# Value projection by rows in four PSUM banks, first weights and activations side by side on one queue, linear-attention head output in the fourth bank

## What is computed

```python
def rmsnorm(x, g):
    xf = x.astype(jnp.float32)
    y = xf * lax.rsqrt(jnp.mean(xf * xf, axis=-1, keepdims=True) + RMS_EPS)
    return (y * g.astype(jnp.float32)).astype(x.dtype)
...
    qkv = jnp.einsum('bsd,de->bse', h, w_qkv).reshape(B, S, 3, N_HEADS, HEAD_DIM)
    q, k, v = qkv[:, :, 0], qkv[:, :, 1], qkv[:, :, 2]
...
    att = jnp.einsum('bnthd,bnshd->bnhts', q_d, k_d)      # linear attention, 4 heads
    att = jnp.where(causal, att, jnp.zeros_like(att))
    o_intra = jnp.einsum('bnhts,bnshv->bnthv', att, v)
...
        o = jnp.einsum('bthd,bhdv->bthv', qc, state)
    o = o_intra + o_inter.transpose(1, 0, 2, 3, 4)
```

## Time and profile before

| what | us |
|---|---|
| median of three runs | 992.41 (991.16 to 992.53) |
| the profiled execution, whole time | 992.35 |
| its span (first to last instruction) | 991.0 |
| PE busy | 982.0, 99% of the span; the chain that ended last is 99% PE |
| DVE busy | 673.7, 68% |
| ACT busy | 578.8, 58% |
| POOL busy | 67.1, 7% |
| DMA, mean over the span | 182 GB/s |

### The profile page before, as it was taken

The page is one execution under the profiler, slowest core; times in us unless marked ns, Lnnn a source line. Parts: engine busy times, 40 slices in busy tenths (PEclk is TensorE's granted clock), DMA queues, the critical chain, the costliest instruction groups (busy, mean ns, idle before and its releaser), DMA issues.

```text
span 991.0 us, 13369 instructions
## 1 busy us (share of the span) xinstructions
PE 982.0 (99%) x5158; PEld 830.4 (84%) x5158; DVE 673.7 (68%) x1143; ACT 578.8 (58%) x1014; POOL 67.1 (7%) x80
## 2 busy tenths in 40 slices
PE   9999999999999999999999999999999999999997
PEld 6887788888888998888888888888888777888886
DVE  6867776655667888766566678778577344667564
ACT  6677755444547896645454575557675434575443
POOL 2223110000000250000000000000120000000000
PEclk9999999999999999999999999999999999999999
DMA  9753545555555445555555556455543433335551
GB/s 368 284 193 139 176 170 204 200 204 179 201 181 174 167 170 177 181 195 186 217 185 198 186 196 228 173 199 181 186 153 129 170 128 132 124 127 197 185 191 43
DMA packets 27263, 180.32 MB, mean 182 GB/s; under 512 B 3008, under 2 KB 3904, under 8 KB 6464
## 3 DMA queue, kind: packets, MB, share of 16 engines
q1 hardware_dynamic: 26336, 176.89, 50.1%
q0 software_dynamic: 288, 2.10, 0.6%
q10 hardware_dynamic: 576, 0.47, 0.2%
HBM read 178.40 MB, written 1.05 MB: 181 GB/s over the span
## 4 chain that ended last, share of the span: by engine, by line
PE 99%; DVE 0%; ACT 0%; issue 0%; DVEq 0%
PE bank L324 25%; PE bank L279 16%; PE bank L281 16%; PE bank L280 16%; PE bank L332 13%; PE bank L294 1%; PE bank L433 1%; PE bank L449 1%; PE bank L552 1%; PE bank L722 1%; PE bank L481 1%; PE bank L295 1%; PE bank L461 1%; PE bank L492 1%; PE bank L425 1%; PE bank L667 0%
## 5 line engine op out<-in xcount | busy, mean ns | idle before, releaser
L1286 DVE TENSOR_TENSOR lo<-raw,hi 128x1024 fp32r<-128x1024 f32 x318 | 376.8, 1231 | 19.3 <-ACT hi L793 19.3
L793 ACT ACTIVATE hi<-raw 128x1024 fp32r<-128x1024 f32 x318 | 320.3, 1050 | 96.0 <-PE bank L281 95.6
L324 PE MATMUL bank<-X,hi 128*128 128x512 f32 x1016 | 266.9, 395 | 0.0
L324 PEld LDWEIGHTS bank<-X,hi 128*128 128x128 f32 x1016 | 185.1, 189 | 33.3 <-issue 0.4
L332 PEld LDWEIGHTS bank<-X,lo 128*128 128x128 f32 x1016 | 138.5, 190 | 10.1
L332 PE MATMUL bank<-X,lo 128*128 128x256 f32 x1016 | 141.6, 282 | 0.0
L824 ACT ACTIVATE bt<-bank 128x256 f32<-128x256 f32 x135 | 51.1, 380 | 147.6 <-PE bank L324 139.4
L1300 DVE TENSOR_TENSOR zr<-bank,bt 128x256 f32<-128x256 f32 x64 | 27.2, 424 | 108.9 <-ACT bt L824 108.9
L279 PE MATMUL bank<-hi,zh 128*128 128x512 f32 x256 | 100.0, 390 | 0.0
L281 PE MATMUL bank<-hi,zl 128*128 128x512 f32 x256 | 99.8, 390 | 0.0
L280 PE MATMUL bank<-lo,zh 128*128 128x512 f32 x256 | 99.6, 389 | 0.0
(11 more groups left out here) (308 smaller groups left out, 1375.8 us busy)
## 6 DMA issues: line engine op xcount, KB each, us to landing
raw<-in_w SPq DMA_DIRECT2D x64, 1024.0 KB, 4.8
raw<-in_rin SPq DMA_DIRECT2D x8, 1024.0 KB, 4.7
raw<-in_wk SPq DMA_DIRECT2D x4, 1024.0 KB, 8.5
raw<-in_wq SPq DMA_DIRECT2D x4, 1024.0 KB, 6.9
raw<-in_wo SPq DMA_DIRECT2D x4, 1024.0 KB, 4.7
raw<-in_mk SPq DMA_DIRECT2D x4, 1024.0 KB, 4.7
raw<-in_mv SPq DMA_DIRECT2D x4, 1024.0 KB, 4.8
raw<-in_rout SPq DMA_DIRECT2D x4, 1024.0 KB, 4.8
```

What stands on the lines that cost most here:

```text
L324: return PE.matmul(bank[b][:, :], wh[:, c:c + P], x[:, k_, :, :].rearrange("p a b -> p (a b)"), start=k_ == 0, stop=k_ == NC - 1, skip_gro ...
L793: ACTE.activation(hi[u_ % HIS][:, c], raw[u_ % RAW][:, c], ACT.Copy).then_inc(hi_cut, 1)
L1286: DVE.tensor_tensor(lo[u_ % RAW][:, c], raw[u_ % RAW][:, c], hi[u_ % HIS][:, c].bitcast(F32), ALU.subtract).then_inc(lo_cut, 1)
```

## The change

It does five things.

1. **Layout.** The `wv` tiles are cut by rows: tile i holds input rows 256 i to 256 i + 255 with all 1024 value columns. For the first four chunks of 128 input rows a new array `front` holds 256 columns of x and 1024 columns of weights side by side. It comes into four tensors `front[0..3]` by five DMAs on SP's queue (384, 256, 640, 640 and 640 KB), then x's chunks 4 to 7 in one DMA, then most of `vec`. Of `vec` only the eight gain columns that the first step reads come on ACT's queue.
2. **Value projection.** `first_rows` takes the place of `first_tokens`: per chunk of input rows twelve matmuls, into banks 0 to 3. `rows` takes the place of `tokens` for tiles 2 and 3. The four value results thus finish together, after the last tile. `wk` 0 and `wq` 0 go to banks (4, 5) and (7, 6).
3. **Order.** ACT cuts the high part of tile 3 before it squares any chunk (before: four squares first). `total` stands on the PE behind all 96 matmuls of the projection (before: 12 ahead of the end). DVE evicts all four results after it has cut the low parts of tiles 4 and 5. `vec_in` is waited for after the squares.
4. **Start.** `warm` is cleared by POOL, and two matmuls run on it instead of four.
5. **Linear attention.** `g_second` writes bank 3, and ACT reads it from there.

The core of the diff:

```diff
-            for k_ in range(4):
-                w, kk = slice(k_ * 512, (k_ + 1) * 512), 4 * t + k_
-                p.wait_ge(first_hi, kk + 1)
+            for j in range(4 * t, 4 * t + 4):
+                kk, c = j // 2, j % 2
+                w = slice(j % 4 * 512, j % 4 * 512 + 512)
+                p.wait_ge(first_hi, j + 1)
                 p.wait_ge(x_low, low_at("mix0", kk))
                 for s_ in range(2):
+                    b = 2 * c + s_
                     if kk == 0:
-                        fill(("wv", 0, s_), banks[s_])
+                        fill(("wv", b), b)
...
         p.wait_ge(warm_set, 1)
-        for i in range(4):
+        for i in range(2):
             PE.matmul(bank[7][:, :], warm[:, 0:P], warm[:, :], start=True, stop=True)
 
-        first_tokens(0, (4, 5))
-        first_tokens(1, (4, 5))
-        tokens("wv", 2, X, (0, 1))
-        tokens("wv", 3, X, (0, 1), (0,))
+        first_rows(0)
+        first_rows(1)
+        for i in (2, 3):
+            rows("wv", i, 4, xh[:, 2 * i:2 * i + 2, :], xl[:, 2 * i:2 * i + 2, :])
         p.wait_ge(ones_in, 16)
         total("mix0", 0)
-        tokens("wv", 3, X, (0, 1), (1,))
         p.wait_ge(ident_in, 16)
-        cols("wk", 0, X2, (2, 3))
-        cols("wq", 0, X2, (4, 5))
-        p.wait_ge(*free["wv", 1, 1])
+        cols("wk", 0, X2, (4, 5))
+        cols("wq", 0, X2, (7, 6))
+        for b in range(4):
+            p.wait_ge(*free["wv", b])
...
-            done = fill(("go", n), 0)
+            done = fill(("go", n), 3)
...
-        ACTE.dma_start(vec[:, :], A["vec"]).then_inc(vec_in, 16)
+        ACTE.dma_start(vec[:, 0:NC], A["vec"][:, 0:NC]).then_inc(gain_in, 16)
         ACTE.preload_act_table_set(LOGS)
+        a.wait_ge(gain_in, 16)
+        for j in range(8):
+            a.wait_ge(first_in[(0, 1, 2, 2, 3, 3, 4, 4)[j]], 16)
+            if j % 2 == 0:
+                high(x_of[j // 2], xh, "norm_mix", j // 2)
+            c, e = j % 4 * 512, S + j % 2 * 512
+            ACTE.activation(hi[j // 4][:, c:c + 512], front[j // 2][:, e:e + 512], ACT.Copy).then_inc(first_hi, 1)
+        a.wait_ge(x_in, 16)
+        for j in (4, 5):
+            high(x_of[j], xh, "norm_mix", j)
+        hi_to(2 * 2 + 2)
+        for j in (6, 7):
+            high(x_of[j], xh, "norm_mix", j)
+        hi_to(2 * 3 + 2)
+        for j in range(NC):
+            square("mix0", x_of, j)
         a.wait_ge(vec_in, 16)
...
-        hi_to(2 * 2 + 2)
-        for j in range(4):
-            square("mix0", hx, j)
-        hi_to(2 * 3 + 2)
-        for j in range(4, NC):
-            square("mix0", hx, j)
...
-        lo_to(2 * (T_OF["wk", 0] + 1))
+        lo_to(2 * (T_OF["wq", 0] + 1))
         by_token("mix0", 1)
         d.wait_ge(tok_made, 1)
-        to_v(0)
-        lo_to(2 * (T_OF["wq", 0] + 1))
-        to_v(1)
+        for n in range(4):
+            s_, r = half_of(n % 2, n // 2)
+            d.wait_ge(*full["wv", n])
+            DVE.tensor_scalar(v[:, s_, r], bank[n][:, :], nst[:, NST["mix0"] + s_:NST["mix0"] + s_ + 1],
+                              None, ALU.mult).then_inc(free["wv", n][0], 1)
...
-        for n in range(3):
-            piece(n)
-            half_tile(n)
-        half_tile(3)
+        for n, (k_, c, e) in enumerate(((0, 0, 3 * S), (0, 3 * S, 5 * S), (1, 0, 5 * S), (2, 0, 5 * S), (3, 0, 5 * S))):
+            SP.dma_start(front[k_][:, c:e], A["front"][:, k_, c:e]).then_inc(first_in[n], 16)
+        SP.dma_start(hx[:, 4:NC, :], A["xT"]).then_inc(x_in, 16)
+        SP.dma_start(vec[:, NC:NV], A["vec"][:, NC:NV]).then_inc(vec_in, 16)
         load(2)
```

More of the change, by code:

```diff
@@ L190, in build @@
     mh, ml = M2[:, :, 0, :], M2[:, :, 1, :]
+    front = [slot("front0", 10, [5 * S]), slot("front1", 10, [5 * S], off=20 * S), slot("front2", 10, [5 * S], off=40 * S),
+             slot("front3", 5, [5 * S])]
+    x_of = [f_[:, 0:S] for f_ in front] + [hx[:, j, :] for j in range(4, NC)]
     q, k, v = slot("q", 5), slot("k", 6), slot("v", 7, [2, D])
@@ L906, in act @@
         at_tile("wv", 2)
+        at_tile("wv", 3)
         inverse_root("mix0")
[L908 removed]
         a.wait_ge(mem_in, 16)
         for j in range(NC):
[L911 removed]
+            high(mem[:, j, :], mh, "g_mem_2", j)
         at_tile("wk", 0)
@@ L941, in act @@
                 if 4 <= j < 8:
-                    square("mem", mem, 2 * (j - 4) + e)
+                    square("mem", [mem[:, n, :] for n in range(NC)], 2 * (j - 4) + e)
         a.wait_ge(*full["av", 7])
@@ L1165, in g_second @@
             a.wait_ge(*full["go", n])
-            ACTE.activation(og[:, :, r], bank[0][:, :].rearrange("p (a b) -> p a b", a=2), ACT.Copy).then_inc(freed[0], 1)
+            ACTE.activation(og[:, :, r], bank[3][:, :].rearrange("p (a b) -> p a b", a=2), ACT.Copy).then_inc(freed[3], 1)
             a.wait_ge(*free["go", n])
@@ L1901, in by_rows @@
             POOL.tensor_tensor(dst[:, j, :], dst[:, j, :], rstd[norm][:, :], ALU.mult).then_inc(done, 1)
+        POOL.memset(warm[:, :], 0.0).then_inc(warm_set, 1)
         sums(0)
```

87 lines of the change are left out of this document (37 added, 50 removed).

## The result

The changed kernel took **989.34 us** (median; 989.21 to 990.51), the kernel before 992.40 us in the same comparison (991.16 to 992.56). The ratio is 0.9975, with an interval of 0.9966 to 0.9985: faster by 0.25%, which is 2.5 us; the medians alone are 3.1 us apart. The profiled execution took 990.01 us and its span is 988.7, against 992.35 and 991.0. The forecast was 989.4. The total came out as forecast. Of the two terms under it the trace bears out one and not the other, and part of the agreement is luck, as the last sections show.

What follows compares the result with a forecast made beforehand. The PE, busy 99% of the span, was taken as the bound, so only its start and waits count. 992.35 less 0.25 (front) and 2.7 (heads) gave 989.4 us, range 987.9 to 990.6.

Steps and rivals of the forecast that it cites:

- the two terms: Gains forecast for the whole kernel: 0.25 us from the earlier start, 2.7 us from the linear attention's heads.
- Step 1: Kernel start: inputs for ACT there at 4.45 us, first real matmul on the PE at 5.5 us.
- Step 2: PE's first matmuls: clock rises from 1.2 to 2.4 GHz at 7.1 us; PE 1.57 us ahead of before.
- Step 3: Value projection, tile 2: PE arrives at 17.1 us and waits 0.2 us, staying 1.4 us ahead of before.
- Step 4: Squares behind tile 3 delay POOL's sums and DVE into the attention; PE's lead over before shrinks to 0.25 us.
- Step 5: Moved `total`, evictions, bank 6 and DMA issue: no added cost, no PE wait at `total`.
- Step 6: Linear attention heads: output in bank 3 removes three PE waits for ACT's read, 0.9 us each, 2.7 us.
- That rival, given 0.13: Kernel start: PE clock stays low until 10.5 us and the lead is gone; 989.7 to 990.2 us, chance 0.13.
- the lead survives: Rival, front into attention: PE keeps its 1.4 us lead over before to the end; 988.2 us, chance 0.2.
- The bank's wait: Rival, between linear attention heads: something else holds the PE, only the front's 0.25 us remains; 992.1 us, chance 0.07.
- Slower: Rival, kernel start: PE clock stays at 1.2 GHz until 20.5 us; 994.4 us or more, chance 0.03.

Runs made afterwards that it cites:

- repetition: The changed kernel timed once more, unaltered, against the kernel before: 989.50 us against 991.57, ratio 0.9981.
- the front alone: The changed kernel with the linear attention's head output back in bank 0, against the kernel before: 991.84 us against 991.89, ratio 1.0002.
- bank 3 alone: The kernel before with only the linear attention's head output moved to bank 3, against the kernel before: 989.64 us against 991.89, ratio 0.9976.

## Why the prediction was right, and where it was not

**Step 1, the start: right.** 5.52 us against 5.5. The first load came 0.2 us sooner (ACT at 4.26, not 4.45), and what released the PE was not `hi` but DVE's `xl`, 0.46 us of waiting; the two cancel. The other estimate, 3.65 us by the fit of the Trainium skill (DMA: Bandwidth & Descriptors, section Anatomy of one DMA), stays open: ACT's row at 4.26 waits for `vec`, so it only says that the front rows were there by then.

**Step 2, the clock: wrong in this execution, and without effect.** It put the rise at 7.1 us and the lead at 1.57. In the profiled execution the lead was 2.2, in its repetition 0.15, in the other traces with two warm-ups between 1.3 and 2.3. The moment is not a property of the kernel, and a single number was too narrow. That rival, given 0.13, did come about in the repetition, lead gone and all; but the time it was to give, 989.7 to 990.2, is where both executions lie (989.76 and 990.01), since neither kept any lead.

**Step 3, tile 2: the place right, the size too small.** 0.34 us of waiting against 0.2, at 17.01 against 17.3; the lead lost 0.6 there in all. That 1.6 were left where 1.4 were forecast is this error set against that of step 2.

**Step 4, the squares: the mechanism right, its end wrong.** Every link was where it was said to be, 0.6 to 0.8 us sooner than forecast: the last square at 24.42 (25.0), tile 4's low part at 26.99 (27.6), tile 6's at 38.55 (39.3), q's join at 41.80 (42.6), the first scores at 43.08 (43.8); no wait at `total`. The 0.6 come from DVE, which was through with tile 3 at 21.15 and not 21.6, so that POOL's first add ended at 21.8 and not 22.3. The PE's waits were 0.3 at `wk` 1 and 0.25 at the scores, not 0.7 and 0.4, and 1.0 us of the lead was left at 44 us, not 0.3.

The step that failed is the sentence behind it: "DVE had 1.2 us idle right behind this place (before 44.63), so it catches up, and the lead that is left goes through to the end". The idle time was used up: k's join stands at 44.03. But DVE then waits 0.65 us for POOL's masking of `T`, a wait that the prediction does not have. Its first softmax step stands at 45.09 against 45.06, its next group at 49.12 against 48.89, and from there on DVE's chain gains nothing, so that the PE's lead melts to -0.2 by 97 us. To be back on the time of before is not to be ahead with the PE. The term was 0.25 and measured -0.2; that falls inside its bounds (-0.3 to 1.4), and the front alone measures as nothing (991.84 against 991.89).

**Step 5, the moves at no cost: right.** No wait at `total`, at the evictions' banks or at bank 6.

**Step 6, the heads: right, a little too large.** 0.9 each was half way between two readings of the rows; measured are 0.84, three times, in the changed kernel and with bank 3 alone: 2.5 us and not 2.7. L685 to L655 is 0.32 us (788.25 less 787.23 and 0.70), inside the 0.35 that were named.

**The sum.** 0.25 + 2.7 = 2.95 were forecast. The traces give -0.2 + 2.5 = 2.3 for the profiled pair, the medians 3.1 in the first comparison and 2.1 in the repetition (991.57 less 989.50). That the median came so close to 989.4 is in part luck. The 992.35 from which the forecast subtracts is one of the slow executions of the kernel before (the medians of three later sets of it are 991.57 to 991.93), and the 2.95 it takes off are 0.6 too many; the two errors go against each other. Both kernels' runs vary by a microsecond or more, which nothing here explains.

**The rivals.** That the lead survives did not happen in the changed kernel; with four squares moved it does (988.3 to 988.6, close to the 988.2 given for it). The bank's wait did not come back. Slower was nowhere near.

## What to carry to other kernels

When one engine is 99% busy and starts earlier, follow the lead to the next place at which two engines hand work to each other in series, and ask for the *other* engine's start there: a lead lives only if every engine in that loop starts earlier. A helper that is busy 68% on average can have nothing to spare for 17 us (DVE here, from 26.99 to 44.44), and what is moved behind a tile (here eight squares, and the sums that hang on them) then comes back in full, a microsecond. Test the two halves of a change alone: here one carried all of it, and the other became worth about a microsecond only when four squares were moved. And before two traces are compared, look for what differs between any two executions: here the landing of one tile (its cut began between 13.8 and 15.6 us) moved the whole chain by as much as some of the edits did.

## What the runs showed of the hardware

**The moment at which the PE's clock rises** differed by microseconds between executions with the same start. In the first trace the real matmuls run at 0.23 us from 5.83 us on, in the repetition at 0.43 us until 9.66, with the same two warm-up matmuls from 1.33 us on and a pause of 0.46 and 0.57 us behind them. The Trainium skill (TensorE: Matmul & The Clock Gate, section The HAM clock gate) says that it shifts from run to run, and the traces agree; the 500 ns either way that it gives in one place are too few for these two, which are some 4 us apart. It cost nothing here, as DVE's chain, late as it was, gave the PE no use for an earlier start.

**Who runs beside whom decides the price of POOL's adds**: seven in 6.66 us when DVE was mostly idle, in 7.86 with one tile's low part beside them, four in 6.87 with low parts beside all of them. It goes the other way too: DVE's low part of 1.22 us took 1.74 at 90 us, and its second scaling 0.76 at 94 us, when POOL's add had started first.
